# An mLSTM block: states before scores, numerators in the staging banks, and a first head prepared earlier

## Time and profile before

| | before |
|---|---|
| median of the runs | 1140.23 us |
| the profiled execution | 1140.49 us, span 1138.7 us |
| PE / PEld busy | 1062.2 us (93%) / 922.4 us (81%) |
| DVE busy | 657.3 us (58%) |
| ACT busy | 530.7 us (47%) |
| POOL busy | 176.2 us (15%) |
| mean granted clock of TensorE | 0.982 of 2.4 GHz |
| moved by DMA | 261.22 MB, mean 229 GB/s |

### The profile page before, as it was taken

One profiled execution on the slowest core, in us unless ns is written; L12 is line 12 of the kernel. 1 busy time (PEld: TensorE's weight loads), 2 busy tenths in 40 slices (PEclk: granted clock), 3 DMA queues, 4 the chain that ended last, 5 costly groups with the idle time before them and its releaser, 6 DMA issues.

```text
span 1138.7 us, 21640 instructions
## 1 busy us (share of the span) xinstructions
PE 1062.2 (93%) x8479; PEld 922.4 (81%) x8479; DVE 657.3 (58%) x959; ACT 530.7 (47%) x862; POOL 176.2 (15%) x247
## 2 busy tenths in 40 slices
PE   5999999889999999999999988898979999999995
PEld 5987878678999999998899845353528989999995
DVE  5567684623485453336996466768684385544333
ACT  5333655514456553425565345353623457553431
POOL 5124000000104220101401530300000104220100
PEclk9999999998999999999999999999999999999998
DMA  9799897997535555444752149898998535544431
GB/s 350 246 340 344 309 332 282 396 403 276 163 124 167 166 166 163 161 161 129 263 167 94 59 144 407 302 402 311 402 342 331 164 125 166 165 157 161 163 129 42
DMA packets 92762, 261.22 MB, mean 229 GB/s; under 512 B 8934, under 2 KB 10086, under 8 KB 92410
## 3 DMA queue, kind: packets, MB, share of 16 engines
q1 hardware_dynamic: 91818, 258.69, 63.7%
q0 software_dynamic: 432, 1.29, 0.4%
q10 hardware_dynamic: 432, 0.14, 0.0%
HBM read 218.36 MB, written 41.73 MB: 228 GB/s over the span
## 4 chain that ended last, share of the span: by engine, by line
PE 79%; DVE 10%; issue 3%; ACT 3%; DMA 2%; SPq 1%; POOL 0%; DVEq 0%; ACTq 0%; POOLq 0%
PE ps L2059 20%; PE ps L2061 20%; PE ps L2060 20%; DVE cring L1761 2%; PE ps L2171 2%; PE ps L2554 2%; DMA w_raw<-in_weights 1%; PE ps L2569 1%; PE ps L2469 1%; PE ps L2431 1%; PE ps L2527 1%; PE ps L2252 1%; PE ps L2153 1%; PE ps L2419 1%; DVE x L1311 1%
## 5 line engine op out<-in xcount | busy, mean ns | idle before, releaser
L1226 DVE TENSOR_TENSOR w_lo<-w_raw,w_hi 128x1024 fp32r<-128x1024 f32 x232 | 285.2, 1236 | 221.4 <-ACT w_hi L710 220.5
L710 ACT ACTIVATE w_hi<-w_raw 128x1024 fp32r<-128x1024 f32 x232 | 242.4, 1055 | 212.5 <-PE ps L2061 176.8
L2059 PE MATMUL ps<-xin_hi,w_hi 128*128 128x288 f32 x1016 | 305.7, 301 | 17.0 <-DVE w_lo L1226 17.0
L2060 PE MATMUL ps<-xin_lo,w_hi 128*128 128x288 f32 x1016 | 302.8, 298 | 0.0
L2061 PE MATMUL ps<-xin_hi,w_lo 128*128 128x288 f32 x1016 | 302.7, 298 | 0.0
L2059 PEld LDWEIGHTS ps<-xin_hi,w_hi 128*128 128x128 f32 x1016 | 192.3, 189 | 29.1 <-DVE w_lo L1226 18.9
L2060 PEld LDWEIGHTS ps<-xin_lo,w_hi 128*128 128x128 f32 x1016 | 192.1, 189 | 0.7
L2061 PEld LDWEIGHTS ps<-xin_hi,w_lo 128*128 128x128 f32 x1016 | 191.6, 189 | 0.0
L2061 PE MATMUL ps<-hid_hi,w_lo 128*128 128x288 f32 x512 | 152.4, 298 | 0.0
L2060 PE MATMUL ps<-hid_lo,w_hi 128*128 128x288 f32 x512 | 152.3, 297 | 0.0
L2059 PE MATMUL ps<-hid_hi,w_hi 128*128 128x288 f32 x512 | 151.3, 296 | 0.0
(11 more groups left out here) (413 smaller groups left out, 1658.4 us busy)
## 6 DMA issues: line engine op xcount, KB each, us to landing
w_raw<-in_weights SPq DMA_DIRECT2D x232, 512.0 KB, 3.4
cring<-in_C SPq DMA_DIRECT2D x64, 512.0 KB, 6.4
out_Cs<-cring SPq DMA_DIRECT2D x64, 512.0 KB, 6.9
kv_a<-in_kv SPq DMA_DIRECT2D x52, 448.0 KB, 5.8
kv_b<-in_kv SPq DMA_DIRECT2D x52, 448.0 KB, 6.0
kv_w<-in_kv SPq DMA_DIRECT2D x24, 448.0 KB, 7.6
out_Cp<-cring SPq DMA_DIRECT2D x8, 512.0 KB, 6.6
out_v<-gaqkv SPq DMA_DIRECT2D x1, 1152.0 KB, 12.8
```

The source lines that it names most:

```text
L710: act.activation(w_hi[:, l % UM], w_raw[:, l % W_SLOTS], ACT.Copy).then_inc(hi_ready, 1)
L1226: dve.tensor_tensor(w_lo[:, l % W_SLOTS], w_raw[:, l % W_SLOTS], w_hi[:, l % UM], ALU.subtract).then_inc(lo_ready, 1)
L2059: pe.matmul(out, w_hi[:, j, ws], hi, start=start and kk == 0, stop=False)
L2060: pe.matmul(out, w_hi[:, j, ws], lo, start=False, stop=False)
```

## The change: what it does

On TensorE a head's round 0 now begins with its states; `sum_groups` of the head before and `scores` follow in round 0's chunk, denominators and numerators in round 1's. The numerators go to two staging banks (`nu0`, `nu1`) and VectorE reads them in round 2, in two halves. `key_sums` moves to round 3 and `row_squares` to round 4, both behind the outer products. `head_rows` moves from round 7 to round 5. The semaphores `num_psum` and `h_ready` go, and with them the waits of banks 4 and 5. On VectorE `new_n` moves to round 4, the norm to rounds 5 and 7, `queries` and `arguments` from round 7 to round 6, `weights` to round 0 of the next head. On ScalarE `head_rows` moves to round 5, `exps` to round 6, the samples' sums to round 0 of the next head. Head 0's queries are made after step 29 of IN_C and its keys after step 30, and the last part of `gate_chain` becomes `gate_outputs`, at step 27.

```diff
-USES = ["q0", "q1", "q2", "q3", "qo", "kt0", "kt1", "ks", "vt0", "vt1", "vs",
-        "bc0", "bc1", "sc", "n", "mean"]
+USES = ["q0", "q1", "q2", "q3", "qo", "kt0", "kt1", "ks", "bc0", "bc1", "vt0", "vt1", "vs",
+        "sc", "nu0", "nu1", "n", "mean"]
-DVE_READS = ("ks", "vs", "sc", "n")
+DVE_READS = ("ks", "vs", "sc", "nu0", "nu1", "n")
@@ scalar engine
             def chunk(h, b):
-                if b == 0:
+                if b == 0 and h:
+                    sample_sums_of(h - 1)
+                if b == 1:
                     act.wait_ge(den_psum, h + 1)
...
-                if b == 1:
-                    act.wait_ge(h_ready, h + 1)
+                if b == 2:
+                    act.wait_ge(stage_read_v, reads(use(h, "nu1"))[1])
                     act.activation(qf[:, :, 0:SEQ], hT, ACT.Square).then_inc(h_sq, 1)
...
+                if b in (3, 4):
+                    prompt_state(h, b - 3)
+                if b == 4:
                     act.activation(dn, staged(h, "mean")[:, 0:SEQ], ACT.Sqrt, bias=tiny[:, 0:1], scale=1.0 / DH
                                    ).then_inc(stage_read_a, 1)
+                    if h + 1 < NH:
+                        qk(h + 1)
...
                 if b == 5 and h + 1 < NH:
                     keys_by_token(h + 1)
                     own_keys(h + 1)
+                    head_rows(h + 1)
                 if b == 6 and h + 1 < NH:
                     values_by_token(h + 1)
+                    exps(h + 1)
+                if b == 7:
                     if h == 2:
                         sample_high(0)
+                    act.wait_ge(hs_psum, h + 1)
+                    act.activation(hs4, ps[:, 2, :], ACT.Copy).then_inc(hs_copied, 1)
-                if b == (6 if h + 1 < NH else 4):
+                if b == (7 if h + 1 < NH else 6):
                     act.wait_ge(y1_full, h + 1)
@@ vector engine
+                if b == 0:
+                    if h:
+                        low_rows(h - 1)
+                    weights(h)
+                if b == 1:
                     dve.wait_ge(den_abs, h + 1)
...
+                if b == 2:
+                    for i in range(2):
+                        src = staged_v(h, f"nu{i}").rearrange("p (c t) -> p c t", t=SEQ)
+                        dve.tensor_tensor(hT[:, 2 * i:2 * i + 2], src, dn.unsqueeze(1).to_broadcast([P, 2, SEQ]), ALU.mult
+                                          ).then_inc(stage_read_v, 1)
...
+                if b == 4:
                     new_n(h)
...
+                if b == 5:
+                    if not last:
+                        keys_low(h + 1)
                     dve.wait_ge(stage_read_a, reads(use(h, "mean"))[1])
                     order.after(dve.reciprocal(dn, dn))
...
+                if b == 6:
+                    if not last:
+                        values_low(h + 1)
+                        queries(h + 1)
+                        arguments(h + 1)
@@ tensor engine
             def chunk(h, b):
                 if b == 0:
+                    if h:
+                        sum_groups(h - 1)
+                    scores(h)
+                if b == 1:
                     denominators(h)
...
                     numerators(h)
+                if b == 3:
+                    key_sums(h)
+                if b == 4:
+                    row_squares(h)
+                    if h + 1 < NH:
                         qk(h + 1)
+                if b == 5:
...
+                    if h + 1 < NH:
                         keys_by_token(h + 1)
                         head_rows(h + 1)
+                if b == 6 and h + 1 < NH:
+                    values_by_token(h + 1)
```

More of the change, by code:

```diff
@@ L1037, in gate_exps, with staged, qk, keys_by_token @@
                 act.activation(gw_c, gw_c, ACT.Exp).then_inc(gact, 1)
+            def staged(h, name):
+                u = use(h, name)
+                act.wait_ge(stage_full, u + 1)
+                return ps[:, 6 + u % 2]
+            def qk(h):
+                for e in range(ET):
+                    act.activation(qf[:, e], staged(h, f"q{e}")[:, 0:T], ACT.Copy, scale=DH ** -0.5
+                                   ).then_inc(stage_read_a, 1)
+                act.activation(qo.rearrange("p e t -> p (e t)"), staged(h, "qo")[:, 0:ET * NS], ACT.Copy
+                               ).then_inc(stage_read_a, 1)
+            def keys_by_token(h):
+                for tt in range(2):
+                    act.activation(ktok[:, tt], staged(h, f"kt{tt}"), ACT.Copy, scale=DH ** -0.5
+                                   ).then_inc(stage_read_a, 1)
             base = STEP0[IN_C]
@@ L1058, in _ @@
                     gate_exps()
[L1061 to L1077, removed]
+                if g == G_PARTS + 7:
+                    qk(0)
+                if g == G_PARTS + 8:
+                    keys_by_token(0)
             act.wait_ge(gcol_ready, 1)
@@ L1811, in sample_rows, with low_rows @@
                 dve.tensor_tensor(rows_f, rows_f, xs, ALU.add).then_inc(y1s_full, 1)
+            def low_rows(h):
+                dve.wait_ge(y1_hi_ready, h + 1)
+                dve.tensor_tensor(y1_lo[:, ET * h:ET * h + ET, 0:SEQ], hT, y1_hi[:, ET * h:ET * h + ET, 0:SEQ],
+                                  ALU.subtract).then_inc(y1_ready, 1)
             def sample_low(c):
@@ L1847, in chunk @@
                     dve.tensor_tensor(hT, hT, z[:, ET * h:ET * h + ET, 0:SEQ], ALU.mult).then_inc(y1_full, 1)
[L1848 to L1871, removed]
+                if b == 7 and last:
+                    low_rows(h)
             dve.wait_ge(gcol_taken, 1)
             keys_low(0)
+            queries(0)
             values_low(0)
-            queries(0)
             arguments(0)
-            weights(0)
             for h in range(NH):
@@ L2390, in gate_columns @@
                 pe.transpose(ps[:, 5, 6 * NH:7 * NH], gw_c[:, SEQ:SEQ + P], four).then_inc(gcol_ready, 1)
[L2392 to L2402, removed]
-                    gate_columns()
             def staged(h, name):
@@ L2446, in keys_by_token @@
                 samples_thrice(h, "ks", 1)
-            qk(0)
-            keys_by_token(0)
+            opening(IN_C, 2)
+            for g in range(OPEN, UM * UNITS[IN_C]):
+                step(IN_C, STEP0[IN_C] + g, g, lambda kk: (xin_hi[:, kk], xin_lo[:, kk]), True, True, None,
+                     None if UM <= g < UM + OPEN else OUT0[IN_C] + g)
+                if g == OPEN + 1:
+                    mean(4)
+                if g == G_PARTS - 1:
+                    gate_products()
+                if g == G_PARTS:
+                    gate_sum()
+                if g == G_PARTS + 7:
+                    qk(0)
+                if g == G_PARTS + 8:
+                    gate_columns()
+                    keys_by_token(0)
             def values_by_token(h):
@@ L2501, in numerators @@
                                      skip_group_check=True)
-                last.then_inc(num_psum, 1)
+                    if e % 2:
+                        last.then_inc(stage_full, 1)
             def key_sums(h):
@@ L2639, in _ @@
                     outers(h, j)
-                    if h + 1 == NH and j + 1 == NB:
-                        sum_groups(h)
                     chunk(h, j)
+            sum_groups(NH - 1)
             sample_turns(1)
```

96 lines of the change are left out of this document (39 added, 57 removed).

## The result

The changed kernel takes 1170.28 us (median of 4 runs, 1167.38 to 1172.72), the kernel before 1140.25 (4 runs, 1136.94 to 1141.66) beside it: a ratio of 1.0267, with a 95% interval of 1.0231 to 1.0302. The forecast was 1169.0 in a range of 1150 to 1180, slower with a chance of 0.87. The profiled execution took 1168.66 us, with a span of 1166.9.

What follows compares the result with a forecast made beforehand. The order of work on four in-order queues was taken to set a head's length. 0.8 + 4.4 + 5.0 + 9.5 gave +19.7 at full clock, plus 9.6 for the clock, on 1140.49: 1169.8, 1169 on the median; range 1150 to 1180.

Steps and rivals of the forecast that it cites:

- The queries' wait: Before the next head's queries, TensorE stands 3.4 us until VectorE's `new_n` in round 4 has read n.
- The hand-over's chain: Between heads, values, queries, arguments, exponentials, then ScalarE's copy of bank 2 end at 16.8 us; TensorE stands 4.85 us.
- The second rows' wait: In the hand-over, the second rows wait 0.7 us for VectorE's read of the sample keys' bank.
- The waits that go: In each head, waits around numerators, outer products, prompt halves and `sum_groups` for `hs4` fall by 2.8 us together.
- The way in: Before head 0, the first outer products start at 657.9 instead of 663.24, -5.3 us; net +0.8 by its round 5.
- The end: From round 5 of head 2 to OUT_C's first matmul: 60.5 us becomes 70.0, +9.5 at full clock.
- The clock at the hand-overs: Half clock after the gap of 4.85 us costs 2.3 us in each of three hand-overs, bounds none to 4.0.
- The clock at the queries: Lower clock at the wait before the queries costs 0.9 us each, three times, bounds 0 to 2.
- Rival 1: The states' stream is the real limit; evenly spaced states shorten heads to 43.7 us, total 1112 to 1126; chance 0.09.
- rival 2's first case: n is read in time, so three times 3.4 us and its clock (2.7) go: 1156; rival 2's chance 0.09.
- Rivals 3 and 4: Clock never falls in a hand-over, 1160, chance 0.16; or stays at half through hand-over and queries, 1178, chance 0.10.
- Rival 5: Nothing on balance: earlier start (5.3) and removed waits (2.8 a head) pay for one surviving wait: 1140; chance 0.04.

Runs made afterwards that it cites:

- the three readings above: VectorE's `new_n` moved from round 4 to round 3 in the changed kernel (1155.94 us, ratio 1.0183): 13.0 us by spans, 9.6 by ratios, 15.7 with the copy moved too.
- The early first head alone: Kernel before with only head 0's queries after step 29, its keys after step 30 and the gate chain in two pieces: 1133.53 us, ratio 0.9972.
- the half stores: Kernel before with one of the two row tiles of each half left out of every state store: 1137.36 us, ratio 1.0014.
- the layout with the earlier norm: Changed kernel with `new_n`, row squares and norm in round 3, queries and arguments earlier, bank 2's copy ahead of exponentials, sample values and `y1_hi`: 1138.53 us, ratio 1.0018.

## Why the prediction was right, by its own steps

The sum was 29.3 us, the difference of the two profiled spans is 28.2. The mechanism was right: TensorE stands where the prediction has it stand, for the reasons that it names, and most waits were right to a few tenths. The clock's terms were less right, and the total owes something to errors that cancel.

- *The queries' wait:* 3.4 predicted, 3.47, 3.46 and 3.53 found. With the clock that goes with it, mending it is worth 10 to 16 us of the 30 by the three readings above.
- *The hand-over's chain:* 16.8 us predicted from round 5's outer products to the end of ScalarE's copy, 16.85 found (694.90 to 711.75). TensorE was done at 12.4 (12.05), so the wait was 4.53 for 4.85, and 4.84 in head 2. The prediction blamed "the exponentials in front of the copy". That part was incomplete: moving them took 2.6 us off TensorE's waits and nothing that the ratio can tell, since VectorE's new states were late by the same queries and arguments. Only both engines' orders together removed the wait (ratio 1.0141 to 1.0083; with the exponentials' place, 1.0183 to 1.0083).
- *The second rows' wait:* 0.7 predicted, 0.54 found. *The waits that go:* 2.8 a head predicted, 2.8 found in head 1 (of the waits of 0.34, 0.98, 1.01, 0.35 and 0.57 before, only 0.43 is left).
- *The way in:* −5.3 predicted, −6.7 found, of which 1.46 stem from before the change; so −5.2. Step 29's wait is gone, as said. Most of it is given back when the scores follow, as predicted, though less (5.7 for 7.0), since head 0's scores ran at the full clock (2.88 us). The early first head alone is worth 2.7 us by the medians, 1.7 by its trace.
- *The end:* 9.5 predicted and 2.3 of clock, 12.3 found. The waits for VectorE's norm and products (2.25 and 4.74) and the 3.15 for the copy behind `y1_hi` are the ones named. Most of it is apart from the hand-overs between the heads: 9.7 us were left when the heads were back at their old distance. `y1_hi` behind the copy took 3.15 of these; the waits for new states stayed (11.2, then 10.5), and the rest of what went is clock.
- *The clock at the hand-overs:* 2.3 each predicted, a choice between 0 and 4.0 for which no row before had such a gap; that it fits is in part luck. Lengths against the same groups at full clock (1.07, 0.73, 1.04, 2.88) give 2.6, 2.1 and 1.6 us.
- *The clock at the queries:* mis-sized. 0.9 each was taken; the queries took 4.18, 3.79 and 3.73 us instead of 2.49, so 1.7, 1.3 and 1.2 on these alone. Not foreseen at all: in heads 2 and 3 the key sums and old states of round 3 ran at half clock after a wait of 2.22 and 1.68 us, another 1.7 each. Head 2's wait for the prompt's copy, 0.6 longer by the prediction, was 0.95 longer (2.22 for 1.27). These account for head 2's 9.1 instead of 8.2.
- *The total:* the three clock terms come to 6.3, 4.2 and 3.4 us, 13.9 for the 9.6 taken; head 0's scores at full clock give back 1.7. The rest of the sum was then some 2 us too high. That 29.3 met 28.2 is partly these two errors cancelling.

The Trainium skill, "TensorE: Matmul & The Clock Gate", section "HAM oscillation — how this bites in real kernels", describes a kernel whose clock falls again after each of its recurring waits (for loads, there). The trace agrees at all six new waits of 3.5 to 4.8 us, though these are for other engines; head 0's scores, after one of 1.99 us, kept the full clock. The clock came back before the hand-over's work was over each time.

Rival 1 (the stream is the limit) is excluded by the half stores for the kernel before, and in the changed kernel no load stands among TensorE's waits; rival 2's first case, for which the prediction had 1156, gave 1155.94 when it was run (by its ratio, 1161 on the runs of the result, so the match to the microsecond is chance). Rivals 3 and 4 were the clock's bounds, 0 and 18; in their terms 10.5 was found (6.3 at the hand-overs, 4.2 at the queries). Rival 5 is what the layout with the earlier norm comes to: with the new waits before the queries gone and those at the hand-overs down to 0.7 us, the new order is worth nothing on balance (1.0018), where the old order with the early first head is at 0.9972.

Two profiles at the same clock show where its gain goes: the half-store run of the kernel before (mean clock 0.988) and this layout (0.987), all scores at 2.88 us in both. From IN_C's wait of 1.68 us to round 5 of head 0 they take 129.9 and 125.4 us, the next two heads 101.7 and 101.6, the end 58.95 and 63.43. So the new layout gains 4.5 us up to head 0's round 5, nothing in the heads between, and loses 4.5 at the end, where TensorE waits for VectorE's new states.

## What to carry to other kernels

Before moving a piece of work, list the buffers that it fills and find for each the place of its reader in the other engine's order: one staging bank read a round late cost 10 to 16 us of 1170. Where a wait is on a chain through two in-order engines, both orders have to be mended; one alone only renames the wait. Count a new gap of several microseconds on TensorE as the gap plus the slow work that follows it (here 3.5 to 4.8 us, and another 1.2 to 2.6 each). And before crediting an edit with a shorter stretch, compare the granted clock and the busy time of the two stretches: of 6.8 us at the end, 3.0 were that.

## What was not expected of the hardware

- The kernel before spreads over 1130.6 to 1144.4 us in the 79 runs beside the experiments, and its mean granted clock goes with it (0.989 at 1130.6, 0.979 at 1144.4; correlation −0.92). In the profiled executions this shows as the scores of a head at 4.57 or at 2.88 us, in the same kernel: heads 1 (4.57) and 3 (2.88) of the earlier trace rows are both, and with the half stores (span 1132.1) all four heads are at 2.88. Three heads at 1.7 each make 5.1 of the 6.6 us between these two spans. Ten runs against 25 still left an interval of 0.24% (2.7 us) to either side.
- Matmuls that keep TensorE busy through a gap hold the clock there (1.00 in 10.4 us), and at the next wait it fell for longer than without them (0.57 against 0.86 over the 12 us from 743; 0.86 also over 746.3 to 758.3, the same place counted from the queries' start). One trace each.
- The narrow matmuls of `key_sums` (one column) and of `old_state` (32 columns) interleave in the records (in head 1 after the change they start at 735.98 and 736.00); in a list by time they look like several groups.
